# A five-layer transformer forward pass: order of score, transpose and pooled-product steps in three attention layers

## The chip, the cores and the metric

The kernel runs on one NeuronCore of a Trainium2 chip, as one launch. The metric is the device time of that launch in microseconds; the median of three runs counts. A profiled execution of the same program gives the trace.

## The reference

One sequence of 512 tokens, width 1024, float32, batch 1. Four layers come first, then one mixed layer with a feed-forward part:

```
for i in range(4):                        # attention kinds 0: MLA, 1: window, 2: fox, 0: MLA
    y = branch(x, ...)                    # (softmax attention * silu(gate)) @ w_out
    x = layernorm(8 ** 0.25 * x + y) * ln_g[i] + ln_b[i]
# fox: 16 heads of 64, causal
s = q @ k.T * 64 ** -0.5 + cum_q - cum_k  # cum: running sum of log_sigmoid(f + b)
# mixed layer
h = rmsnorm(x); z = h @ w_in
ya = b * causal_conv3(c * a)              # 256 channels
yb = pool_w @ (trailing mean(2, 4, 8, 16) - token) * pool_scale
yc = attention over the top 128 keys by a small indexer, 4 heads, relative bias
yd = attention over blocks (here: all causal keys), 4 heads, relative bias
x = x + rmsnorm(concat(ya, yb, yc, yd) @ w_out)
x = x + rmsnorm(swiglu(rmsnorm(x))); x = x + sigmoid(rmsnorm(x) @ wg) * (p @ wp)
```

The window layer (16 query heads, 4 key heads) sees 128 keys back and adds a per-head slope and a sink to the softmax.

## The kernel before

All activations stay on the chip. Each matrix is held as a rounded high part and a low part (`XTh`, `XTl` and so on), and each product is three products (high by high, low by high, high by low). Weights come in units of 512 KB at most: SyncE loads `w_raw`, ScalarE rounds it to `w_hi` (L1382), GpSimd subtracts to get `w_lo` (L2856). A "tile" is the product of one unit with the transposed tokens, 24 matmuls of 512 columns (L532), whose result goes to one of two projection banks in turn; ScalarE writes its high half, VectorE its low half, and only then is the bank free for the tile after next.

There is no scheduler. The program is written once for each engine, and each engine's list runs in the order in which it is written, with semaphores between them. A change of order on one engine must have its counterpart on the others.

Attention goes by pairs of heads, one head in each half of the array's rows. `pair_attention` on TensorE runs i from -2 to the last pair. In iteration i it takes the transposes of pair i, the scores of pair i+2, the product with V of pair i (`mix`, L772), and the layer's `fill(i, pos)`, which adds tiles for later pairs. The steps have numbers:

```
if n % 2:
    scores(i + 2, n // 2)
else:
    turn(i, n // 2)
```

`turn(i, ch)` (L758) transposes 14, 14 and 12 blocks of the probabilities into banks 4 and 5; it waits for the norm of these probabilities and for ScalarE's copy of the group before (L1537). `scores(i, ch)` (L716, and L728 for fox's bias rows, L732 for the mask of selected keys) writes two banks, 0 and 1 or 2 and 3 in turn, and waits with `ps_free` until VectorE has emptied the chunk before the last:

```
if c.sch >= 2:
    pe.wait_ge(ps_free, c.sch - 1)
```

A causal pair has three chunks: query rows 2 and 0 together, row 3, row 1 (with selection row 1 before row 3). In the window layer there are two chunks and two groups of transposes. `between(i)` says which steps come before the fills (a list) and which are woven into the tiles of fill 1 and 2 (a dictionary: point of weaving to steps; a tile has a point after every three matmuls, a value half after each eight). The third score chunk comes behind the fills, just ahead of `mix(i)`.

VectorE's `pair_attention` (L2206) empties a chunk with a custom operation that adds the bias and finds the maxima (L2227, `maxima`). The result goes to the buffer that pair i's probabilities lie in, so for the first chunk it waits, for each head, for pair i's transposes:

```
if ch == 0 and i >= 2:
    dve.wait_ge(pt_done, t_first[i - 2] + pr.turns_of(x))
```

`turns_of` is 2 for the first head and 3 for the second (1 and 2 in the window layer). Then come the norms of pair i+1 (L2254 and L2256; in the mixed layer only the reciprocal, L2252, and ScalarE does the multiplication, L1527), the gates (L2113), and the product of attention and gate (L2271). `norm_last` and `norm_first` move the second head's norm behind the fills and the mix, or ahead of them.

ScalarE takes in iteration i, in this order: copies of all groups of transposes of pair i (L1537), the high half of the output, exponentials of pair i+1, first head (L1512), a rounding of weights, second head, then norms and high halves of tiles. In the fox layer each score needs augmented rows (the running sums), moved by four small transfers from ScalarE's queue (L1892) right behind the gate tile of the iteration before; `scores` waits for them at its first chunk.

In the mixed layer `pooled(cc)` is a float32 product of the pooled channels (L1189) that waits for GpSimd's window sums (L2811 to L2820); VectorE scales it into `otmp` (L2698), ScalarE writes the high half and VectorE the low half. VectorE also finds the selected keys in rounds of eight (`top`, L2666 and L2667). In the condition `pairs[0].sel` the first pair is asked; only pairs 2 and 3 of the mixed layer select.

## Time and profile before

| | |
|---|---|
| runs | 1652.9 us median of 3 (1652.37 to 1653.56) |
| profiled execution | 1657.83 us |
| its span | 1656.0 us |
| mean granted TensorE clock | 0.995 |
| busy: TensorE, VectorE, ScalarE, GpSimd | 98%, 47%, 46%, 40% |
| chain that ended last: TensorE, VectorE, ScalarE | 80%, 11%, 5% |

The profile is one execution, seen by the hardware profiler. Times in its views are from the start of the span. A row of a timeline is a start, a duration, the engine with the line of the kernel, the operation, the tiles written and read, and in brackets how long the engine stood idle before it and who ended that. Matmuls overlap, so the distance between two starts is what one costs, not its duration. "PE" is TensorE, "DVE" VectorE, "ACT" ScalarE, "POOL" GpSimd; "ACTq" is ScalarE's queue issuing a transfer.

The fox layer's pairs lie between 470 and 700 us of the span, the window layer's between 280 and 415, the mixed layer's between 1099 and 1190.

### The profile page before, as it was taken

Reading aid. Unit: us, or ns where it says so; the run is one execution under the profiler, and the core shown is the slowest. Engines: PE = TensorE matmul, PEld = TensorE weight load, DVE = VectorE, ACT = ScalarE, POOL = GpSimd, SP = SyncE. Lnnn points to the kernel's source line nnn. Section 1 sums busy time; section 2 is a strip of 40 time slices with the busy share of each in tenths; the row PEclk is TensorE's granted clock in tenths of the full one; section 3 lists DMA queues with packets and bytes.
Section 4 is the critical chain, followed back from the end, with each engine's and each line's share of the span. In section 5 each row is a group of like instructions: output and inputs, shape, how many; then the busy total and the mean of one; then the engine's idle time right before and its main releaser. Section 6 shows DMA issues by size and latency. Waiting matters only on the chain.

```text
span 1656.0 us, 26230 instructions
## 1 busy us (share of the span) xinstructions
PE 1620.8 (98%) x10245; PEld 1313.5 (79%) x10245; DVE 776.0 (47%) x2044; ACT 757.8 (46%) x1465; POOL 658.2 (40%) x551
## 2 busy tenths in 40 slices
PE   8999999999999999999999999999999999999998
PEld 7777778887888787788777788777688888888877
DVE  3778635665543434354877464886051111001162
ACT  4566624655345444434576534328553322213252
POOL 5332234332443333243423243882235444444423
PEclk9999999999999999999999998999999999999999
DMA  6323144233452323153312265231243333333412
GB/s 174 71 45 87 52 161 125 80 83 60 160 157 55 85 56 93 58 194 79 88 41 75 73 184 152 79 90 56 90 135 102 102 91 101 102 92 97 120 62 89
DMA packets 216071, 161.32 MB, mean 97 GB/s; under 512 B 53763, under 2 KB 197155, under 8 KB 215948
## 3 DMA queue, kind: packets, MB, share of 16 engines
q1 hardware_dynamic: 205904, 130.21, 28.1%
q10 hardware_dynamic: 9820, 29.40, 5.7%
q8 instruction: 82, 1.34, 0.3%
q14 instruction: 41, 0.34, 0.1%
q0 software_dynamic: 224, 0.03, 0.1%
HBM read 148.32 MB, written 11.14 MB: 96 GB/s over the span
## 4 chain that ended last, share of the span: by engine, by line
PE 80%; DVE 11%; ACT 5%; issue 2%; POOL 2%; DMA 1%; SPq 0%; DVEq 0%; ACTq 0%; POOLq 0%
PE banks L532 40%; PE banks L483 8%; PE banks L485 7%; PE banks L484 7%; PE banks L772 4%; PE banks L716 4%; PE banks L614 4%; PE banks L758 3%; PE banks L738 1%; DVE banks L2354 1%; ACT AB L1512 1%; DVE banks L2343 1%; DVE AB L2356 1%; ACT w_hi L1382 1%; ACT G L1634 1%
## 5 line engine op out<-in xcount | busy, mean ns | idle before, releaser
L2856 POOL TENSOR_TENSOR w_lo<-w_raw,w_hi 128x512 fp32r<-128x512 f32 (+2 forms) x506 | 617.5, 1248 | 968.0 <-ACT w_hi L1382 967.7
L1382 ACT ACTIVATE w_hi<-w_raw 128x1024 fp32r<-128x1024 f32 (+4 forms) x254 | 249.8, 994 | 158.7 <-PE banks L485 102.0
L532 PE MATMUL banks<-XTh,w_hi 128*128 128x512 f32 (+5 forms) x1216 | 283.6, 375 | 7.2 <-DVE XTl L2316 3.0
L532 PE MATMUL banks<-XTl,w_hi 128*128 128x512 f32 (+5 forms) x1216 | 274.0, 367 | 0.0
L532 PE MATMUL banks<-XTh,w_lo 128*128 128x512 f32 (+5 forms) x1216 | 272.4, 367 | 0.0
L532 PEld LDWEIGHTS banks<-XTh,w_hi 128*128 128x128 f32 (+2 forms) x1216 | 209.0, 190 | 53.7 <-issue 8.3
L532 PEld LDWEIGHTS banks<-XTl,w_hi 128*128 128x128 f32 (+2 forms) x1216 | 212.7, 189 | 37.8
L532 PEld LDWEIGHTS banks<-XTh,w_lo 128*128 128x128 f32 (+2 forms) x1216 | 212.7, 189 | 37.4
L483 PE MATMUL banks<-w_hi,OTh 128*128 128x512 f32 (+1 forms) x448 | 172.8, 386 | 1.6 <-DVE QKl L2080 1.5
L484 PE MATMUL banks<-w_lo,OTh 128*128 128x512 f32 (+1 forms) x448 | 167.8, 375 | 0.0
L485 PE MATMUL banks<-w_hi,OTl 128*128 128x512 f32 (+1 forms) x448 | 167.7, 374 | 0.0
L1512 ACT ACTIVATE AB<-AB,nb 128x256 f32<-128x256 f32 (+3 forms) x288 | 152.5, 533 | 13.0 <-DVE nb L2237 13.0
L1537 ACT ACTIVATE AB<-banks 128x896 f32<-128x896 f32 (+1 forms) x100 | 89.0, 890 | 116.7 <-PE banks L758 116.7
L2256 DVE TENSOR_SCALAR_CACHE_REDUCE AB<-AB,ri 128x256 f32<-128x256 f32 (+3 forms) x256 | 118.2, 518 | 2.3
L2227 DVE CUSTOM_DVE_ANT_0 AB<-banks,zmask 128x384 f32<-128x384 f32 (+1 forms) x192 | 84.0, 487 | 58.2 <-PE banks L758 53.8
L2747 DVE TENSOR_TENSOR otmp<-banks,AB 128x512 f32<-128x512 f32 x22 | 15.2, 692 | 188.9 <-PE banks L532 188.9
L483 PEld LDWEIGHTS banks<-w_hi,OTh 128*128 128x128 f32 x448 | 84.2, 188 | 22.2 <-DVE QKl L2080 3.3
L2080 DVE TENSOR_TENSOR QKl<-banks,QKh 128x512 fp32r<-128x512 f32 (+2 forms) x80 | 54.4, 683 | 100.0 <-ACT QKh L1411 98.6
L485 PEld LDWEIGHTS banks<-w_hi,OTl 128*128 128x128 f32 x448 | 84.3, 188 | 15.5
L484 PEld LDWEIGHTS banks<-w_lo,OTh 128*128 128x128 f32 x448 | 84.4, 188 | 13.6
L1411 ACT ACTIVATE QKh<-banks 128x512 fp32r<-128x512 f32 (+2 forms) x80 | 46.8, 586 | 80.4 <-PE banks L532 64.5
L758 PEld LDWEIGHTS banks<-ident,AB 64*128 64x128 f32 x1344 | 50.4, 138 | 22.4 <-issue 19.7
(222 smaller groups left out, 2209.6 us busy)
## 6 DMA issues: line engine op xcount, KB each, us to landing
w_raw<-in_w_gate_up_dram SPq DMA_DIRECT2D x44, 512.0 KB, 3.8
w_raw<-in_fox_w_in_dram SPq DMA_DIRECT2D x30, 512.0 KB, 4.1
w_raw<-in_mla_w_in_dram SPq DMA_DIRECT2D x26, 512.0 KB, 4.9
w_raw<-in_w_in_dram SPq DMA_DIRECT2D x24, 512.0 KB, 4.0
w_raw<-in_w_down_dram SPq DMA_DIRECT2D x22, 512.0 KB, 3.6
w_raw<-in_swa_w_in_dram SPq DMA_DIRECT2D x20, 512.0 KB, 3.8
w_raw<-in_mla_w_out_dram SPq DMA_DIRECT2D x16, 512.0 KB, 3.2
x_spill<-AB ACTq DMA_DIRECT2D x16, 512.0 KB, 2.8
```

The source lines that it names most:

```text
L483: nc.tensor.matmul(o, ah, bh, start=first, stop=False, skip_group_check=True)
L484: nc.tensor.matmul(o, ah, bl, start=False, stop=False, skip_group_check=True)
L485: return nc.tensor.matmul(o, al, bh, start=False, stop=last, skip_group_check=True)
L532: mm = nc.tensor.matmul(o, wt[:, k, :], xt[:, k, lo:hi], start=first and n == 0 and k == 0, stop=last and n == 2 and k == nk - 1, skip_gro ...
L614: mm = nc.tensor.matmul(o[:, 256 * (t % 2):256 * (t % 2) + 256], xt[:, k, ts], parts[k // 4][low][:, k % 4, :], start=n == 0 and k == 0, s ...
L758: mm = nc.tensor.transpose(bank[4 + half][:, o:o + HD], SBP[a % 2][m // n][r, col:col + P], ident[r, r])
L1382: nc.scalar.activation(view(w_hi, u, RING), view(w_raw, u, RAW), ACT.Copy).then_inc(hi_done, 1)
L1512: ins = nc.scalar.activation(sc, sc, ACT.Exp, bias=nb[:, b, n0 + t:n0 + t + 1], scale=pr.scale, accum_out=rs[:, b, n0 + t:n0 + t + 1])
L1537: nc.scalar.activation(PTB[:, P * m0:P * m1].rearrange("p (n h q) -> p h n q", h=2, q=HD), banks[:, 4:6, 0:HD * n].rearrange("p h (n q) -> ...
L2227: ins = nc.vector.tensor_tensor_reduce(pr.score(b, x, t), o, pr.bias(t, x), 1.0, -3e38, ALU.add, ALU.max, mx[:, b, 4 * x + t:4 * x + t + 1])
L2256: ins = nc.vector.tensor_scalar(pr.score(b, x, t), pr.score(b, x, t), ri[:, b, 4 * x + t:4 * x + t + 1], None, ALU.mult, ALU.add, accum_ou ...
L2856: ins = pool.tensor_tensor(low[at], raw[at], high[at].bitcast(F32), ALU.subtract)
```

## The change

Six edits. (1) In `between`, fox pairs 0 to 5 take the second score chunk before the second group of transposes, and the third group of transposes and the third score chunk are woven into the first tile of the fills; a set keeps the third chunk from being issued twice. (2) The condition for the mixed layer asks the last pair, so that pairs 0 and 1 weave their second and third transposes and the second score chunk into a tile. (3) At the mixed layer's next to last pair the woven transposes come at points 1 and 2 instead of 2 and 4. (4) The second pooled product moves behind the query tile of pair 1 and the first two score chunks of pair 0, on TensorE, ScalarE and VectorE. (5) VectorE in the window layer does the second head's norm of i = 5 last. (6) A list holds the group count that the output product waits for.

```diff
--- before.py
+++ after.py
@@ -776,8 +776,12 @@
                     end(mm)
                     mixed_at[a] = c.g
 
+                scored = set()
+
                 def step(i, n):
 
+                    if n == 5:
+                        scored.add(i)
                     if n % 2:
                         scores(i + 2, n // 2)
                     else:
@@ -786,11 +790,13 @@
                 def between(i):
 
                     if i == n_pairs - 2:
-                        return [0], {2: [2], 4: [4]}
+                        return [0], {1: [2], 2: [4]} if pairs[i].sel else {2: [2], 4: [4]}
                     if pairs[0].window:
                         return ([0], {3: [2, 1, 3]}) if i == 0 else ([0, 1, 3, 2], {})
-                    if pairs[0].sel and i >= 0:
+                    if pairs[-1].sel and i >= 0:
                         return [0, 1], {1: [2, 3], 3: [4]}
+                    if pairs[0].aug is not None and 0 <= i < n_pairs - 2:
+                        return [0, 1, 3, 2], {2: [4, 5]}
                     return list(range(5)), {}
 
                 for i in range(-2, n_pairs):
@@ -825,7 +831,8 @@
                     fill(i, 2)
                     woven.pop()
                     assert i == n_pairs - 1 or not later
-                    scores(i + 2, 2)
+                    if i not in scored:
+                        scores(i + 2, 2)
                     mix(i)
                     fill(i, 3)
                 c.pair += n_pairs
@@ -1201,16 +1208,17 @@
             tile("pool")
             mark["pool", 1] = c.g
             pair_values(0)
-            pooled(1)
-            at_mixed = c.g
-
-            parts = []
+
+            parts, at_mixed = [], []
 
             def fill(i, pos):
                 if pos == 0:
                     if i < 1:
                         pair_tile("q", i + 3)
                 elif pos == 1:
+                    if i == -2:
+                        pooled(1)
+                        at_mixed.append(c.g)
                     if i < 1:
                         pair_tile("k", i + 3)
                     elif i == 1:
@@ -1231,7 +1239,7 @@
                 return OTh[:, OUT_ORDER[k], ts], OTl[:, OUT_ORDER[k], ts]
 
             def chunk_at(k):
-                return at_mixed if k < 4 else mixed_at[c.pair - 8 + k]
+                return at_mixed[0] if k < 4 else mixed_at[c.pair - 8 + k]
 
             pe.wait_ge(idx_r, 24)
             pair_attention(rel_pairs(), fill, mixed_ahead)
@@ -2009,15 +2017,16 @@
             hi(OTh[:, 2, :], otmp[:, :])
             pool_tile(1)
             value_units(1)
-            c.g += 1
-            groups_stored(act, c.g)
-            hi(OTh[:, 3, :], otmp[:, :])
 
             def fill(i, pos):
                 if pos == 0:
                     if i < 1:
                         pair_tile(i + 3)
                 elif pos == 1:
+                    if i == -2:
+                        c.g += 1
+                        groups_stored(act, c.g)
+                        hi(OTh[:, 3, :], otmp[:, :])
                     if i < 1:
                         pair_tile(i + 7)
                     elif i == 1:
@@ -2572,7 +2581,7 @@
                     gate(i + 1)
                     gate_at[i + 1] = c.g
 
-            pair_attention(swa_pairs(), fill, norm_first=(-1,))
+            pair_attention(swa_pairs(), fill, norm_last=(5,), norm_first=(-1,))
             ln_tail(1)
             for rows in (QKh, QKl):
                 for half in range(2):
@@ -2714,7 +2723,6 @@
             c.g += 1
             top(13)
             c.g += 2
-            pooled(1)
             dve.wait_ge(rel_in, 16 * 32)
             dve.wait_ge(x_out, 16 * T * 4)
 
@@ -2727,6 +2735,8 @@
                     elif i == 2:
                         c.g += 1
                 elif pos == 1:
+                    if i == -2:
+                        pooled(1)
                     if i < 0:
                         top(2)
                     if i < 1:
```

The order on TensorE, fox layer, one of the six pairs (L758 transposes, L716 and L728 scores, L532 the tile). Before:

```order
L728 MATMUL banks<-QKh 128x128 x2
L758 MATMUL banks<-ident,AB 128x64 x14
L716 MATMUL banks<-QKh 128x512 x2
L716 MATMUL banks<-QKl,QKh 128x512 x2
L716 MATMUL banks<-QKh,QKl 128x512 x2
L728 MATMUL banks<-QKh 128x512 x2
L758 MATMUL banks<-ident,AB 128x64 x12
L532 MATMUL banks<-XTh,w_hi 128x512 x8
```

and now:

```order
L728 MATMUL banks<-QKh 128x512 x2
L758 MATMUL banks<-ident,AB 128x64 x14
L532 MATMUL banks<-XTh,w_hi 128x512 x6
L758 MATMUL banks<-ident,AB 128x64 x12
L716 MATMUL banks<-QKh 128x256 x2
L716 MATMUL banks<-QKl,QKh 128x256 x2
L716 MATMUL banks<-QKh,QKl 128x256 x2
L728 MATMUL banks<-QKh 128x256 x2
L532 MATMUL banks<-XTh,w_hi 128x512 x2
```

The 12 transposes of the third group moved six matmuls into the tile, and the scores of 256 columns, which stood behind the tiles, follow them directly.

The order on TensorE, mixed layer, pair 0, from its second group of transposes on (L732 adds the mask of the selected keys):

```order
L532 MATMUL banks<-XTh,w_hi 128x512 x3
L758 MATMUL banks<-ident,AB 128x64 x14
L716 MATMUL banks<-QKh 128x256 x2
L716 MATMUL banks<-QKl,QKh 128x256 x2
L716 MATMUL banks<-QKh,QKl 128x256 x2
L732 MATMUL banks<-OTl,ident_r 128x256 x2
L532 MATMUL banks<-XTh,w_hi 128x512 x5
L532 MATMUL banks<-XTl,w_hi 128x512
L758 MATMUL banks<-ident,AB 128x64 x12
L532 MATMUL banks<-XTl,w_hi 128x512 x7
```

Before, both groups of transposes and the chunk between them stood ahead of the tile.

The order on VectorE, window layer, i = 5 (L2122 is the gate, L2280 the product of attention and gate, L2259 to L2265 the norm):

```order
L2122 SCALAR_TENSOR_TENSOR G<-G,banks 128x512
L2280 SCALAR_TENSOR_TENSOR otmp<-banks,G 128x512
L2259 TENSOR_TENSOR rs<-rs,es 128x4
L2263 RECIPROCAL ri<-rs 128x4
L2265 TENSOR_SCALAR AB,unused<-AB,ri 128x128
L2265 TENSOR_SCALAR AB,unused<-AB,ri 128x256 x3
```

Before, the last four of these rows stood ahead of the first two.

## Rows read from the trace of the kernel before

**Rows 1.** The page's first part: busy time of each engine (share of the span) and instructions.
```profile
PE 1620.8 (98%) x10245; PEld 1313.5 (79%) x10245; DVE 776.0 (47%) x2044; ACT 757.8 (46%) x1465; POOL 658.2 (40%) x551
```

**Rows 2.** List of waits of TensorE: waiter, releaser, us in total, times, longest.
```profile
PE banks L758 <- ACT AB L1537: 0.9, 3, 0.3
```

**Rows 3.** Timeline of TensorE, fox pairs 0 to 2: start us, us, engine, line, operation.
```profile
545.72 0.39 PE L716 MATMUL banks<-QKh 64*128 64x256 f32 x2
...
546.39 2.37 PE L772 MATMUL banks<-AB,V 128*64 128x512 f32 x16
548.69 0.65 PE L758 MATMUL banks<-ident,AB 64*128 64x64 f32 x14
549.22 0.44 PE L716 MATMUL banks<-QKh 64*128 64x384 f32 x2
...
551.66 0.41 PE L728 MATMUL banks<-QKl 64*128 64x512 f32 x2
552.20 0.59 PE L758 MATMUL banks<-ident,AB 64*128 64x64 f32 x12
552.72 2.11 PE L532 MATMUL banks<-XTh,w_hi 128*128 128x512 f32 x8
...
572.23 0.65 PE L758 MATMUL banks<-ident,AB 64*128 64x64 f32 x14
572.72 0.44 PE L716 MATMUL banks<-QKh 64*128 64x384 f32 x2
```

**Rows 4.** Timeline of VectorE in fox pair 1: S0's second half.
```profile
552.83 0.56 DVE L2227 CUSTOM_DVE_ANT_0 AB<-banks,zmask 128x384 f32<-128x384 f32 x1 [0.80 <-PE banks L758]
...
553.52 0.08 DVE L2227 DVE_READ_ACCUMULATOR2_ANT mx<- 128x1 f32 x1
```

**Rows 5.** Timeline of VectorE and TensorE at fox's first pairs: a score group that waits.
```profile
505.84 0.08 DVE L2227 DVE_READ_ACCUMULATOR2_ANT mx<- 128x1 f32 x1
...
505.98 0.50 PE L716 MATMUL banks<-QKh 64*128 64x512 f32 x2 [0.39 <-DVE mx L2227]
```

**Rows 6.** Timeline of ScalarE's queue: the last transfer of augmented rows of two pairs.
```profile
547.37 0.48 ACTq L1892 DMA_DIRECT2D QKl<-OTl  x1
...
570.91 0.48 ACTq L1892 DMA_DIRECT2D QKh<-OTl  x1
```

**Rows 7.** Timeline of VectorE and TensorE, sliding-window layer, i = 5 and 6.
```profile
391.42 0.54 DVE L2250 TENSOR_TENSOR rs<-rs,es 128x4 f32<-128x4 f32 x1 [1.03 <-ACT es L1515]
...
393.68 0.68 DVE L2113 SCALAR_TENSOR_TENSOR G<-G,banks 128x512 f32<-128x512 f32 x1
...
394.51 1.63 PE L532 MATMUL banks<-XTh,w_hi 128*128 128x512 f32 x6 [1.74 <-DVE G L2113]
396.07 0.65 PE L758 MATMUL banks<-ident,AB 64*128 64x64 f32 x14
```

**Rows 8.** Timeline of TensorE: the second pooled product.
```profile
1098.36 1.10 PE L1189 MATMUL banks<-AB 128*128 128x512 f32 x2 [1.31 <-POOL AB L2820]
```

**Rows 9.** Timeline of TensorE, ScalarE and VectorE, mixed layer, pairs 0 and 1.
```profile
1135.89 0.59 PE L758 MATMUL banks<-ident,AB 64*128 64x64 f32 x12 [0.27 <-ACT AB L1537]
...
1137.23 0.39 ACT L1512 ACTIVATE AB<-AB,nb 128x128 f32<-128x128 f32 x1
...
1142.71 1.92 ACT L1527 ACTIVATE AB<-AB,ri 128x128 f32<-128x128 f32 x4
1143.65 2.37 PE L772 MATMUL banks<-AB,V_odd 128*64 128x512 f32 x16
...
1145.22 0.69 DVE L2080 TENSOR_TENSOR QKl<-banks,QKh 128x512 fp32r<-128x512 f32 x1 [2.37 <-ACT QKh L1411]
...
1145.96 0.65 PE L758 MATMUL banks<-ident,AB 64*128 64x64 f32 x14
1146.42 0.42 PE L716 MATMUL banks<-QKh 64*128 64x384 f32 x2
...
1147.30 0.90 ACT L1537 ACTIVATE AB<-banks 128x896 f32<-128x896 f32 x1
```

**Rows 10.** Timeline of ScalarE and TensorE, mixed layer: the mix of pair 2.
```profile
1170.26 0.58 ACT L1434 ACTIVATE V<-banks 128x512 f32<-128x512 f32 x1
...
1170.93 3.88 PE L772 MATMUL banks<-AB,V 128*64 128x512 f32 x16 [2.45 <-issue]
```

**Rows 11.** Stretches: length, busy us (instructions) of PE, PEld, DVE, ACT, POOL; PEclk, DMA share, GB/s.
```profile
1001.00:1013.00 12.00, 12.00 (x59) 11.96 (x57) 2.87 (x5) 4.34 (x7) 5.01 (x4) 0.50 0.55 160
...
1171.00:1173.00 2.00, 2.00 (x6) 0.75 (x8) 0.00 (x0) 2.00 (x9) 1.93 (x2) 0.50 0.00 0
```

## Prediction

> **What bounds the kernel now.** I read the page first: TensorE is busy for 1620.8 us of 1656.0, 98% [rows 1]. So every gain is a TensorE wait removed, and every new TensorE wait is paid in full. The list of waits shows them small; the transposes that wait for ScalarE's copies lose 0.9 us in three places [rows 2]. Then I read timelines at the four places that the change touches. I call a pair's three groups of transposes T0, T1, T2 (steps 0, 2, 4 of pair i), the score chunks of pair i+2 S0, S1, S2 (steps 1, 3, and 5 or the call behind the fills), and the product with V "mix".
>
> In the fox layer TensorE never stands still for long: S2, mix, T0, S0, T1, S1, T2, then three tiles, one pair in 23.54 us from T0 to T0 (548.69 to 572.23) [rows 3]. What is to be seen there is who is close behind. S2 may start only when VectorE has emptied the banks of S0, the same two banks, since it waits for all score chunks but the last one. VectorE may empty the second head's half of S0 only when T2 is done, since it overwrites what T2 reads: its row at 552.83 starts after T2 and its last read ends at 553.60 [rows 4]. Today S2 comes 13 us later, so nobody notices. A score group that does wait for VectorE begins 0.06 us after such a read ends, 505.92 to 505.98 [rows 5]. And S0 of the next pair begins a fixed time after the last small ACT transfer of the augmented rows was issued: 547.37 to 549.22 and 570.91 to 572.72, that is 1.85 and 1.81 us [rows 3, 6]. So S0 already starts when that transfer lands. TensorE fills the 3.50 us from the end of the gate tile (545.72) to S0 with S2 (0.67), mix (2.30) and T0 (0.53) [rows 3].
>
> **The change part by part.**
>
> *Fox, six pairs (i = 0 to 5).* T0, S0, S1, T1, six matmuls of the first tile, T2, S2, rest. T2 is followed at once by S2. From T2's start VectorE begins 0.63 us later (552.20 to 552.83), needs 0.77 and wakes TensorE in 0.06: S2 starts 1.46 us after T2 instead of the 0.52 after which the tile now follows [rows 3 to 5]. That is 0.94 of new wait, six times. Back comes T2's present wait for ScalarE's copy of T1: S1's last two matmuls start at 551.66 and stream for some 0.23, T2 starts at 552.20, of which an ordinary switch is 0.1; I take 0.2 [rows 3]. The number of switches between tiles, scores and transposes stays eight a pair. T1 now leads into a tile; 12 transposes before a tile take 0.52, 14 before scores 0.46 [rows 3, 9], so I add 0.1. Net 0.94 - 0.2 + 0.1 = 0.84 a pair, 5.0 us for six. If VectorE were early by everything but its second half the wait would still be 0.7, if it had gated work ahead of it some 1.1: 3.6 to 6.6.
>
> Second, S2 no longer lies between the gate tile and the next S0. The transfers are issued from the same point, the end of the gate tile, so S0 stays 3.50 us behind it, and the 0.67 that S2 took there becomes idle time while S2's work is paid elsewhere. This holds for the pairs whose rows are fetched right before use and with no value tile between: after i = 0, 1, 3, 4. Four times 0.67 is 2.7 us; nothing at least, 3.2 at most. The Trainium skill, "DMA: Bandwidth & Descriptors", section "Anatomy of one DMA", gives some 2.0 us of fixed cost for a transfer on the GpSimd path; by that S0 would be held another 0.15 to 0.2 longer and the sum would be 0.7 higher. The rows have 1.85 and 1.81 for this queue, so they decide. Fox in sum: +7.7 us.
>
> *Sliding-window layer.* At i = 5 VectorE norms the second head before it finishes the gate (393.68), and TensorE's last gate tile waits 1.74 us for the bank at 394.51 [rows 7]. Now the gate comes first. The tile can start at about 392.75, behind T0, but T1 inside it (now 396.07) needs that norm, which starts behind the gate and the mix product at about 393.15 instead of 391.42 and still needs some 2 us: T1 at 395.2. Gain 0.9 of the 1.74; between 0.4 and 1.7. Queued behind the norm on VectorE is only the low half of the output, which waits for ScalarE anyway.
>
> *Second pooled product.* It waits 1.31 us for GpSimd's window sums at 1098.36 [rows 8]. Behind a query tile and two score chunks (over 7 us of work) the sums are done; the product itself moves and costs the same. VectorE's scale and subtraction move behind five selection rounds and the maxima; they are short and VectorE is the same length ahead of the selected scores. The key tile that follows now needs the bank of the query tile, which VectorE empties some 0.3 us before TensorE comes. -1.3, between -1.4 and -0.5.
>
> *Mixed layer, pairs 0 and 1.* The branch for them was dead before (it asked the first pair, which selects nothing) and lives now: T1 and S1 after three matmuls of the tile, T2 after nine. T2 of pair 0 comes 2.2 us later. But ScalarE copies all three groups before it turns to the next pair's exponentials, and it is busy without a break from T2's copy on: exponentials at 1137.23, norm 1142.71 for 1.92, so it needs 8.74 us from T2 (1135.89) to the norm at 1144.63, while TensorE's T0 of the next pair comes at 1145.96, 10.07 after T2 [rows 9]. With T2 2.2 later (and a switch more) TensorE is back after 8.0 and waits 0.8. S0 behind it waits for the low half of the key (1145.22 + 0.69, 10.0 us after T2) and loses another 0.8. At pair 1 the same shift costs T0 of pair 2 some 1.2, and its T1, now after one group of the value tile, waits for ScalarE's copy of T0, which ends about 11 us after the exponentials begin (1137.23 to 1148.20) [rows 9]: 1.9. The last mix, which waits 2.45 today because ScalarE's V copy at 1170.26 comes behind copies and exponentials [rows 10], is down to 0.7, since T2 of pair 2 comes two groups nearer to the tile's start. New waits 0.8 + 0.8 + 1.2 + 1.9 + 0.7 = 5.4, old ones 0.3 + 0.3 + 0.3 + 2.45 = 3.3, four more switches 0.6: +2.7, between -1.5 and +4.
>
> *The clock there.* In the stretch behind the 2.45 us of idling the granted clock is 0.50, the 1.2 GHz level, and the mix took 3.88 us instead of 2.37 at full clock [rows 9 to 11]. With the idle time cut into pieces I expect the clock to hold 2.4 GHz: -1.5. "TensorE: Matmul & The Clock Gate" of the Trainium skill, section "Part 1: The HAM clock gate", says that the clock follows how busy the engine was just before, not any one wait. By that rule two waits close together could bring it down as well, and the sum would be 1.5 higher; this is a rival below.
>
> **Sum.** +7.7 - 0.9 - 1.3 + 2.7 - 1.5 = +6.7 us. The profiled execution took 1657.8; it would be 1664.5. The runs' median is 1652.9, 4.9 below it, and the forecast for the median is 1659.6.
>
> **Rivals.** (1) *Fox as forecast, mixed pays off.* If ScalarE has more room than I give it, the mixed order costs nothing (-1.3 - 1.5 - 1) and the sum is about +3, 1656. For it: the old idle was 3.3 us and the longest piece shrinks. Against it: ScalarE has no gap in its rows there. (2) *The transfers hide.* Only the bank wait of S2 counts, fox +5.0: 1656.9. Against: the two equal distances of rows 3 and 6. (3) *Clock.* The waits of 1.2 and 1.9 us before T0 and T1 of pair 2 lie within 5 us and the clock falls there as it does today: +1.5, 1661.1. (4) *S2 never waits: not slower.* VectorE's emptying of S0 keeps up with TensorE. Its place is the start of S2 in the six fox pairs, its price the 0.94 each (5.6 in all), and it decides once the wait is under 0.3. The sum is then +1.1, 1654.0, no change that can be measured. For it: VectorE is idle before T2. Against: it can't begin before T2 ends, and the six matmuls of tile lie ahead of T2, not between T2 and S2. (5) *The slow stretch at 1000.* Between 1001 and 1013 the granted clock is 0.50 as well, behind short matmuls and small waits [rows 11]. If the later arrival kept the clock up there, half of that stretch, 6 us, would come back: +0.7, 1653.6. Against: the runs before agree within 1.2 us, so it falls there each time.
>
> **How the numbers follow.** Runs of this kernel spread by 1.2 us, so under 0.2% (3.3 us) I call it the same. Forecast 0.5, rival 1 0.13, rival 2 0.1, rival 3 0.12, rival 4 0.1, rival 5 0.05. Rival 1 lies on the bound: 0.045 of it counts as slower, 0.065 as the same, 0.02 as faster. Of the forecast 0.02 ends within the bound. Rival 4 is 0.06 the same and 0.04 faster, where the transfers hide too; rival 5 is the same. Rounded: slower 0.74, same 0.19, faster 0.07. The range takes in all but rivals 4 and 5 and the far ends: the fox bounds alone reach from 3.6 to 9.8, the others shift that by -3 to +1; 1654.5 to 1662.5.
>
> **What would show it.** In the timeline of fox pairs: T2's first transpose to S2's first matmul 1.4 to 1.5 us with VectorE's maxima as releaser, and T0 to S0 1.2 us after i = 0, 1, 3, 4, with a period of 25.0 us instead of 23.5. In the window layer the wait of 1.74 gone and one of under 1 us before T1. The pooled product without a wait. Mixed: TensorE waits before T0 and S0 of the later pairs and before T1 of pair 2, ScalarE without gaps, clock 1.0 at the last mix. The forecast is wrong if S2 follows T2 within 0.6 us or the fox period is not over 24 us.

## The result and the profile after

The changed kernel is slower. In the runs taken together with the result its median is 1665.1 us against 1652.8 (four runs each; ratio 1.0074, 95% interval 1.0050 to 1.0098). Those four runs lie in two pairs, 1661.7 and 1661.9, 1668.2 and 1668.4. With eight more executions (last experiments) the median of twelve is 1662.1: seven lie at 1659.9 to 1662.2, five at 1668.1 to 1668.5. The prediction was 1659.6 with 1662.5 as its upper end.

The page's busy line, beside [rows 1], says little: TensorE is busy 3.2 us longer in a span that is 10.6 us longer (1666.6 against 1656.0).

```profile
PE 1624.0 (97%) x10245; PEld 1316.4 (79%) x10245; DVE 773.8 (46%) x2044; ACT 757.7 (45%) x1465; POOL 658.8 (40%) x551
```

The list of TensorE's waits says more (waiter, releaser, us in total, times, longest). The wait for VectorE's maxima was there once before, for 0.4 us, that for ScalarE's copies with 0.9 us in total, and that of the mix (L772) was longer, 2.5 us; the others are new:

```profile
PE banks L716 <- DVE mx L2236: 5.6, 7, 0.9
...
PE banks L758 <- ACT AB L1545: 1.9, 1, 1.9
...
PE banks L772 <- issue: 1.7, 1, 1.7
PE banks L716 <- DMA QKl<-OTl: 1.5, 2, 1.0
PE banks L758 <- ACT AB L1535: 1.5, 2, 1.1
...
PE banks L716 <- DMA QKh<-OTl: 1.2, 2, 0.7
...
PE banks L758 <- DVE AB L2265: 0.8, 1, 0.8
...
PE banks L716 <- DVE QKl L2089: 0.6, 1, 0.6
```

The timeline of TensorE in fox pair 1, which answers to [rows 3]:

```profile
546.46 2.38 PE L772 MATMUL banks<-AB,V 128*64 128x512 f32 x16
548.77 0.65 PE L758 MATMUL banks<-ident,AB 64*128 64x64 f32 x14
550.38 0.44 PE L716 MATMUL banks<-QKh 64*128 64x384 f32 x2 [0.96 <-DMA QKl<-OTl]
...
554.67 0.58 PE L758 MATMUL banks<-ident,AB 64*128 64x64 f32 x12
556.13 0.39 PE L716 MATMUL banks<-QKh 64*128 64x256 f32 x2 [0.88 <-DVE mx L2236]
...
574.33 0.65 PE L758 MATMUL banks<-ident,AB 64*128 64x64 f32 x14
575.51 0.44 PE L716 MATMUL banks<-QKh 64*128 64x384 f32 x2 [0.53 <-DMA QKh<-OTl]
```

From T2 (554.67) to S2 (556.13) it is 1.46 us, and the releaser is VectorE. From T0 to S0 it is 1.61 and 1.18 us, where it was 0.53 and 0.49. The period is 25.56 us instead of 23.54. VectorE's own rows answer to [rows 4]: it begins the second half 0.63 us after T2 starts, and its last read ends 0.05 us before S2.

```profile
555.30 0.56 DVE L2236 CUSTOM_DVE_ANT_0 AB<-banks,zmask 128x384 f32<-128x384 f32 x1 [1.22 <-PE banks L758]
...
555.99 0.09 DVE L2236 DVE_READ_ACCUMULATOR2_ANT mx<- 128x1 f32 x1
```

The last transfers of augmented rows, which answer to [rows 6], are issued at 548.11 and 573.67; S0 follows 2.27 and 1.84 us behind:

```profile
548.11 0.48 ACTq L1900 DMA_DIRECT2D QKl<-OTl  x1
...
573.67 0.48 ACTq L1900 DMA_DIRECT2D QKh<-OTl  x1
```

In the sliding-window layer the wait of 1.74 us is gone and one of 0.76 stands before T1 [rows 7]; the pooled product now runs without a wait [rows 8]:

```profile
392.87 1.63 PE L532 MATMUL banks<-XTh,w_hi 128*128 128x512 f32 x6
395.25 0.65 PE L758 MATMUL banks<-ident,AB 64*128 64x64 f32 x14 [0.76 <-DVE AB L2265]
...
1113.70 1.12 PE L1196 MATMUL banks<-AB 128*128 128x512 f32 x2
```

The mixed layer's pairs, TensorE's rows with their waits, beside [rows 9, 10]:

```profile
1154.19 0.65 PE L758 MATMUL banks<-ident,AB 64*128 64x64 f32 x14 [0.37 <-ACT AB L1535]
1155.46 0.44 PE L716 MATMUL banks<-QKh 64*128 64x384 f32 x2 [0.63 <-DVE QKl L2089]
...
1169.90 0.65 PE L758 MATMUL banks<-ident,AB 64*128 64x64 f32 x14 [1.10 <-ACT AB L1535]
...
1173.57 0.79 PE L758 MATMUL banks<-ident,AB 64*128 64x64 f32 x14 [1.88 <-ACT AB L1545]
...
1183.03 2.38 PE L772 MATMUL banks<-AB,V 128*64 128x512 f32 x16 [1.74 <-issue]
```

Two stretches run at 1.2 GHz, as in [rows 11], but the first is longer and the second lies elsewhere: 17.1 us from 1006.7 on (13.7 us from 999.9 on before), and 3.4 us at T1 of pair 2 instead of at the last mix (the starts and lengths are those of the trace's record of the granted clock; the rows lie inside them; stretch: length, busy us of PE, PEld, DVE, ACT, POOL; PEclk, DMA share, GB/s).

```profile
1007.00:1023.00 16.00, 16.00 (x87) 15.77 (x87) 2.87 (x5) 4.34 (x7) 4.99 (x4) 0.50 0.50 144
1174.00:1177.00 3.00, 3.00 (x27) 2.66 (x24) 0.00 (x0) 0.92 (x1) 0.00 (x0) 0.50 0.00 0
```

**Where the 10.6 us came in**, by the same point of the program in both traces:

| from, to | before, us | after, us | difference |
|---|---|---|---|
| start to T0 of fox pair 0 | 525.14 | 524.33 | -0.8 |
| to T0 of fox pair 6 | 153.78 | 162.33 | +8.6 |
| to the indexer's first scores (3.4 us more at half clock) | 340.81 | 342.49 | +1.7 |
| to T0 of mixed pair 0 (the pooled product is in here) | 112.42 | 110.93 | -1.5 |
| to the first transposes behind the last mix | 45.58 | 48.21 | +2.6 |

The sum is +10.6; behind the last point nothing changes. The first line contains the window layer; the executions of one kernel differ by some 0.7 us there (525.04 in a second trace of the changed kernel), so its -0.8 is good to about that.

### The profile page after: what moved, and what is told of

Same layout as the page of the kernel before. It is cut to its first block, busy times and chain, and to the rows that moved or that the text cites. A ratio compares the mean times of both kernels' runs of the same rounds, so it can differ in the third digit from the quotient of the medians.

```text
span 1666.6 us, 26230 instructions
## 1 busy us (share of the span) xinstructions
PE 1624.0 (97%) x10245; PEld 1316.4 (79%) x10245; DVE 773.8 (46%) x2044; ACT 757.7 (45%) x1465; POOL 658.8 (40%) x551
## 4 chain that ended last, share of the span: by engine, by line
PE 80%; DVE 10%; ACT 5%; issue 2%; DMA 1%; POOL 1%; ACTq 0%; SPq 0%; DVEq 0%; POOLq 0%
PE banks L532 41%; PE banks L483 8%; PE banks L485 7%; PE banks L484 7%; PE banks L716 4%; PE banks L614 4%; PE banks L772 3%; PE banks L758 3%; ACT AB L1520 1%; PE banks L738 1%; DVE banks L2363 1%; DVE banks L2352 1%; DVE AB L2365 1%; ACT w_hi L1390 1%; ACT G L1642 1%
## 5 line engine op out<-in xcount | busy, mean ns | idle before, releaser
L532 PE MATMUL banks<-XTh,w_hi 128*128 128x512 f32 (+5 forms) x1216 | 284.9, 376 | 5.5 <-DVE XTl L2325 3.0
L532 PE MATMUL banks<-XTl,w_hi 128*128 128x512 f32 (+5 forms) x1216 | 275.1, 368 | 0.0
L532 PE MATMUL banks<-XTh,w_lo 128*128 128x512 f32 (+5 forms) x1216 | 273.3, 368 | 0.0
L532 PEld LDWEIGHTS banks<-XTh,w_hi 128*128 128x128 f32 (+2 forms) x1216 | 208.4, 190 | 51.8 <-issue 6.6
L532 PEld LDWEIGHTS banks<-XTh,w_lo 128*128 128x128 f32 (+2 forms) x1216 | 213.7, 190 | 37.4
L532 PEld LDWEIGHTS banks<-XTl,w_hi 128*128 128x128 f32 (+2 forms) x1216 | 213.2, 190 | 38.0
L2265 DVE TENSOR_SCALAR_CACHE_REDUCE AB<-AB,ri 128x256 f32<-128x256 f32 (+3 forms) x256 | 118.2, 518 | 2.3
L758 PEld LDWEIGHTS banks<-ident,AB 64*128 64x128 f32 x1344 | 51.3, 139 | 25.2 <-issue 19.3
```

What stands on the lines that cost most here:

```text
L532: mm = nc.tensor.matmul(o, wt[:, k, :], xt[:, k, lo:hi], start=first and n == 0 and k == 0, stop=last and n == 2 and k == nk - 1, skip_gro ...
L758: mm = nc.tensor.transpose(bank[4 + half][:, o:o + HD], SBP[a % 2][m // n][r, col:col + P], ident[r, r])
L2265: ins = nc.vector.tensor_scalar(pr.score(b, x, t), pr.score(b, x, t), ri[:, b, 4 * x + t:4 * x + t + 1], None, ALU.mult, ALU.add, accum_ou ...
```

## Experiments

**The fox order alone, and everything but it.** The new fox order was put into the kernel before:

```diff
+                    if pairs[0].aug is not None and 0 <= i < n_pairs - 2:
+                        return [0, 1, 3, 2], {2: [4, 5]}
...
-                    scores(i + 2, 2)
+                    if i not in scored:
+                        scores(i + 2, 2)
```

> The kernel before with the new order of the fox layer alone (the pooled product, the sliding-window layer and the mixed layer as before). Theory: the fox layer carries nearly all of the loss, about +8.5 us against before: six waits of S2 for VectorE's emptying of S0's banks (T2 to S2 1.45 us instead of 0.52, some 5.4 us) and a longer idle time before the next S0 behind four pairs (some 3.2 us). Rival A (the mixed layer's new order is the larger part): not over +5. Rival B (the whole loss is the granted clock of the mixed layer, which only reacts to a later arrival): the fox rows show waits, but the time comes out within 3 us of before.

Measured: 1668.2 us against 1653.0 (ratio 1.0074, interval 1.0052 to 1.0096; here and below the ratio is the recorded one over all executions, which with two levels is not the quotient of the medians); five of six executions at 1668.1 to 1669.1, one at 1660.9. In its trace T0 of pair 0 to T0 of pair 6 takes 162.22 us, +8.4, with the same waits. Taking the two lines out of the changed kernel was the counterpart:

> The changed kernel with the fox layer in its old order. Theory: the window layer gives 0.8 back, the pooled product 1.3, the mixed pairs cost 2.7: +0.6 us against before, between -1 and +2. Rival A (mixed layer is the larger part): +4 to +6.

Measured: 1652.7 against 1653.0 (interval 0.9982 to 1.0012). The rest of the change comes out even within this interval, though not by the forecast parts: in this trace the mixed part takes 49.45 us, +3.9, with the clock at 1.2 GHz for 6.8 us of it. Rivals A and B are out: the fox layer carries the larger part of the loss in rows of its own, and with the fox order alone the mixed part is what it was (45.66 us).

**The two fox costs taken apart.** In the first version S2 comes late in the tile, in the second it goes back between the gate tile and the mix:

```diff
-                        return [0, 1, 3, 2], {2: [4, 5]}
+                        return [0, 1, 3, 2], {2: [4], 5: [5]}
```

> The kernel before with the new fox order, but S2 behind 15 matmuls of the first tile instead of right behind T2 (6 matmuls). Theory: VectorE has emptied the banks by then, so the six waits of 0.87 us are gone; S2 still does not lie between the gate tile and the next S0, so the idle time before S0 of 1.2 to 1.6 us stays in four pairs: +3 us against before, between +2 and +4.5. Rival C (both losses come from T1 standing behind S0 and S1, which puts ScalarE and VectorE late): +7 or more, as with the full order.

```diff
-                        return [0, 1, 3, 2], {2: [4, 5]}
+                        return [0, 1, 3, 2], {2: [4]}
```

> The kernel before with T0, S0, S1, T1 and then T2 inside the first tile, but S2 in its old place between the gate tile and the product with V. Theory: neither the bank wait nor the longer idle time before S0, and T2's old wait of 0.2 us for ScalarE's copy is gone: -1 us against before, between -2 and +0.5. Rival C: +4 or more.

S2 late: the fox part takes 158.39 us, 3.8 less than with the full order and 4.6 more than before. All waits of the six pairs for VectorE's maxima are gone; what is left there is in the list of waits of this stretch:

```profile
PE banks L716 <- DMA QKh<-OTl: 1.4, 2, 0.8
PE banks L716 <- DMA QKl<-OTl: 1.1, 2, 0.5
PE banks L614 <- ACT w_hi L1389: 0.6, 1, 0.6
```

So the transfers are exposed in four pairs with no bank wait about. +3 was expected and +4.6 came: 2.5 are the idle time for the transfers, 0.6 is a weight copy that is late for a value tile, and the last 1.5 falls to what is left, among it one more switch into and out of a tile in each of six pairs; that share was not measured apart. S2 in its old place: fox takes 155.68 us, +1.9, where I expected -1. No bank wait, but one transfer that lands late (1.1 us, behind i = 3) and the weight copy (0.8). The sign is right (rival C is out), the size was not: the order of T1, S1 and T2 gains nothing. The medians of these two, 1662.8 and 1662.6, are of no use for this, since 7 and 10 of their 12 executions lie on a high level, of which more below; their low executions (1655.4 to 1657.9, and 1654.4 and 1654.8) agree with the traces.

**The parts of the mixed layer.** First the order of pairs 0 and 1 alone, then pair 2's alone, in the kernel before:

```diff
-                    if pairs[0].sel and i >= 0:
+                    if pairs[-1].sel and i >= 0:
```

> The kernel before with only the new order of the mixed layer's pairs 0 and 1 (T1, S1 and T2 inside the query tile and the key tile), pair 2 as before. Theory: ScalarE is behind, so T0 and S0 of pair 1 wait 0.4 and 0.6 us and T0 of pair 2 waits 1.1: the part from T0 of pair 0 to T0 behind the last mix grows by 1.5 to 3 us against before. Rival D (the cost lies in pair 2's earlier T1 alone): this part does not grow by over 0.5 us.

```diff
-                        return [0], {2: [2], 4: [4]}
+                        return [0], {1: [2], 2: [4]} if pairs[i].sel else {2: [2], 4: [4]}
```

> The kernel before with only pair 2 of the mixed layer in its new order (T1 after one group of the value tile, T2 after two). Theory: ScalarE's weight split stands ahead of its V copy and waits for the value tile's last product, so the last mix still waits 1.7 us instead of 2.45; T1 waits under 0.5 us since T0 is not late here: this part shrinks by 0.3 to 1 us. Rival E (the weight split is not what holds it, the earlier T2 makes the V copy early): wait at the last mix 0.7 us or less, the clock stays at 1.0 there, -3 us.

Pairs 0 and 1: the part takes 48.27 us against 45.58, +2.7, with waits of 0.36, 0.63, 1.10 and 0.92 us before T0, S0, T0, T1 and still 2.45 before the last mix; the median is 1655.6 against 1652.9. Rival D is out: this edit has the whole cost of the mixed layer in these traces. Pair 2 (median 1656.4, seven of twelve executions high; ratio 0.9998, interval 0.9981 to 1.0015): 43.61 us, 2.0 less, but in this execution the clock held and the mix took 2.38 instead of 3.88 us, so the order itself gives some 0.5. The wait at the last mix is 1.74, as expected.

**Pooled product and window layer alone**, the edits as in the change:

> The kernel before with only the second pooled product moved and the gate ahead of the norm in the sliding-window layer. Theory: -0.8 (window layer) and -1.5 (pooled product), so 2.3 us faster than before where the granted clock falls as often. Rival F (the pooled move only shifts the wait into the key tile behind it): -0.8.

Measured: 1648.9 against 1652.9 (ratio 0.9969, interval 0.9953 to 0.9985), faster than both kernels, and by 1.7 us more than the two edits are worth. The stretch at the last mix, after the same wait of 2.45 us, has most of it:

```profile
1163.00:1167.00 4.00, 3.64 (x22) 2.38 (x23) 0.18 (x1) 4.00 (x13) 2.36 (x2) 1.00 0.21 38
```

The granted clock is 1.00 here and was 0.50 in [rows 11], and the mixed part takes 44.04 us instead of 45.58. One and the same wait brings the clock down in one execution and not in another. The window layer may add to it: behind its old wait of 1.74 us before the gate tile the clock falls for 3.4 us in four of the nine traces that have this wait (the fox order alone, T2 alone, pair 2 alone, the delayed kernel below), and T0 of fox pair 0 then comes some 1.1 us later; in none of the eight traces with the new order there does it fall. Nine and eight traces are too few to call this shown.

**What holds the last mix.** ScalarE's V copy comes behind a weight split that reuses a buffer of the value tile. I tried to exchange the two in the layer's fill:

```diff
                     elif i == 1:
-                        advance()
                         values(0)
+                        advance()
```

> A version that might beat both: the kernel before with the pooled product moved, the gate ahead of the norm, pair 2 of the mixed layer in its new order, and ScalarE's V copy of that pair put ahead of the weight split. Theory (the weight split sets the last mix's wait): that wait falls from 1.7 to about 0.6 us, the clock holds 2.4 GHz there, and with the other two parts the kernel is 4 to 6 us faster than before. Rival E (the split is not what holds it): the wait at the last mix is the same as with the order of pair 2 alone, and the time 2.5 us under before.

Measured: 1648.5 us, and the wait is still 1.74. The order on ScalarE there had not moved:

```profile
1161.38 1.06 ACT L1383 ACTIVATE w_hi<-w_raw 128x1024 fp32r<-128x1024 f32 x1 [1.10 <-PE banks L614]
1162.35 0.58 ACT L1435 ACTIVATE V<-banks 128x512 f32<-128x512 f32 x1
```

The split is issued by the pair's own steps. So that was changed instead:

```diff
-                    if not c.early and 0 <= i < n_pairs - 1:
+                    if not c.early and 0 <= i < n_pairs - 1 and not (pairs[i].sel and i == n_pairs - 2):
                         early()
```

> The version with the pooled product moved, the gate ahead of the norm and pair 2 of the mixed layer in its new order (no new fox order, pairs 0 and 1 as before), and now ScalarE's weight split of that pair really behind its V copy: the split is issued inside the pair's own steps, so exchanging it with the copy in the fill had moved nothing. Theory (the split, which waits for the value tile's last product and takes 1.06 us, sets the start of the last mix): the wait there falls from 1.74 to 0.8 us and the part from T0 of pair 0 to T0 behind the last mix from 43.6 to 42.6 us. Rival E (something else holds the mix): 1.74 us as before.

The V copy now starts when the value tile ends and the mix waits 0.73 us (timelines of ScalarE and TensorE):

```profile
1160.44 0.60 ACT L1435 ACTIVATE V<-banks 128x512 f32<-128x512 f32 x1 [1.03 <-PE banks L614]
1160.93 1.05 ACT L1383 ACTIVATE w_hi<-w_raw 128x1024 fp32r<-128x1024 f32 x1
...
1161.14 2.37 PE L772 MATMUL banks<-AB,V 128*64 128x512 f32 x16 [0.73 <-issue]
```

The part takes 42.56 us instead of 43.61, as expected. Right behind it 0.59 of this is lost again: T1 of the last pair now waits for ScalarE's copy of T0 (1168.16), which comes behind a norm of 3.72 us and is no earlier than TensorE. The median is 1647.8 against 1652.8 (ratio 0.9972, interval 0.9956 to 0.9987), 0.6 below the version before it, a difference that 11 and 8 executions don't clear of noise.

**The two levels.** Each version so far has executions some 5 to 8 us above the others, with a mean granted clock of 0.992 to 0.996 instead of 0.997 to 1.000. In the seven traces of high ones the stretch at half clock near 1005 us is there, in the ten others not. Two tests: does a later arrival alone change how often it falls, and do the waits ahead of it cause it?

```diff
+                for _ in range(again):
+                    nc.tensor.matmul(o, h[:, 0, :], XTh[:, 0, lo:hi], start=True, stop=False, skip_group_check=True)
...
-                    tile("gate")
+                    tile("gate", again=8 if i == -1 else 0)
```

> The kernel before with eight matmuls of the first fox gate tile repeated (its first matmul, same operands and same result, start flag set each time), so that everything behind it comes 1.8 us later and nothing else changes. It tests why the stretch of half clock near 1000 us appears in some executions and not in others. Theory G (it is chance in relation to the time of arrival, so the fox order raises its share only by coming later): about +1.8 us on the fast executions, and the share of executions that lie 5 to 7 us higher differs clearly from the kernel before's, near the 10 of 12 of the version with T2 alone moved, whose fox layer was 1.9 us longer. Rival H (the fox order itself does it): the share stays near the kernel before's 16 of 60.

```diff
-                for _ in range(3):
-                    open_half("iq", P)
+                for n in range(3):
+                    open_half("iq", P, again=4 if n == 2 else 0)
                 turn(2)
-                open_half("ik")
+                open_half("ik", again=9)
```

> The changed kernel with the TensorE waits at the start of the mixed layer filled: in the layer's early column groups the first matmul of the third and of the fourth group (256 columns) is repeated 4 and 9 times with the same operands, which takes the place of the waits of 0.56 and 1.20 us there. Theory (those waits, together with the short matmuls, pull the clock down): the half-clock stretch of 13 to 17 us near 1005 is gone in nearly all executions and the median lies at the changed kernel's lower level, 1661 to 1662 us. Rival J (the short matmuls alone do it, or something outside the kernel): the share of high executions is as in the changed kernel.

> The changed kernel itself once more, to have more executions of it beside the others: two levels as in its first four runs, about 1661.8 and 1668.3 us, with over half of the executions on the higher one.

> The kernel before with the two waits at the start of the mixed layer filled by repeated matmuls as in the filled version of the changed kernel. Theory (the waits pull the clock down there in some executions): the kernel before lay 5 to 8 us high in 22 of 86 executions; here none or one of 12 does, the rest at 1650.4 to 1653.8 as before. Rival J (the waits have nothing to do with it): about 3 of 12 high.

> The kernel before with the new fox order alone, waits at the start of the mixed layer filled. With the waits it lay on the high level in 5 of 6 executions (1668.1 to 1669.1), once at 1660.9. Theory: none or one of 12 high, the median at 1660 to 1661.5, so the fox order costs 8 us in work and waits and the rest of its 15 us was the clock. Rival H (the fox order itself causes the high level, wherever the clock falls): over half of the executions near 1668.

> The fastest version so far (pooled product moved, gate ahead of the norm, pair 2 in its new order, V copy ahead of the weight split; 1646.8 to 1648.6 in 8 executions and 1652.7 to 1653.2 in 3) with the waits filled. Theory: the high level goes, median 1647 to 1648, none above 1650. Rival J: 3 of 12 at 1653 as without.

| version | executions on the high level | median, us |
|---|---|---|
| before | 27 of 111 | 1652.7 to 1653.0 |
| changed kernel with the old fox order | 2 of 12 | 1652.7 |
| order of pairs 0 and 1 alone | 4 of 12 | 1655.6 |
| order of pair 2 alone | 7 of 12 | 1656.4 |
| pooled product and window layer alone | 2 of 12 | 1648.9 |
| these two and pair 2's order | 2 of 8 | 1648.5 |
| before, delayed by 1.8 us in fox | 7 of 12 | 1661.0 |
| before, waits filled | 0 of 12 | 1652.9 |
| fox order alone | 5 of 6 | 1668.2 |
| fox with S2 late | 7 of 12 | 1662.8 |
| fox with S2 in its old place | 10 of 12 | 1662.6 |
| fox order alone, waits filled | 0 of 10 | 1659.5 |
| changed kernel | 5 of 12 | 1662.1 |
| changed kernel, waits filled | 0 of 6 | 1661.8 |
| fastest version without fox order | 3 of 11 | 1647.8 |
| the same, waits filled | 0 of 10 | 1647.1 |

The stretch of 20 us at this place in the fox order alone, and in the same with the waits filled:

```profile
1005.00:1025.00 20.00, 18.79 (x111) 18.31 (x110) 6.15 (x10) 5.78 (x10) 4.99 (x4) 0.61 0.42 119
```

```profile
1005.00:1025.00 20.00, 19.69 (x164) 18.52 (x162) 8.68 (x14) 10.96 (x22) 9.55 (x8) 1.00 0.49 136
```

TensorE gets through 164 matmuls in it instead of 111; the repeated ones lie ahead of this stretch. And in the filled one the wait of 1.20 us has shrunk to 0.16, since VectorE sets its end and not TensorE (timeline of TensorE, kernel before with the waits filled):

```profile
993.43 1.27 PE L529 MATMUL banks<-XTh,w_hi 128*72 128x256 f32 x9
...
997.68 1.11 PE L534 MATMUL banks<-XTh,w_hi 128*128 128x128 f32 x8 [0.16 <-DVE XTl L2318]
```

The four versions have no high execution in 38 with the waits filled, and 40 in 140 without. So the waits of 0.56 and 1.20 us are shown to be needed for the fall; they were filled together, and which of them counts was not tried. Rival J is out, and so is rival H of the filled fox version: with the waits filled no execution at 1668 is left. The medians put the fox order at 6.6 to 6.8 us then (1659.5 against 1652.9 filled and 1652.7 unfilled). The two filled traces, in which the clock does not fall at all before the last microseconds, have 7.8 us between their spans (1656.5 and 1648.7).

What raises the share is not shown. The versions with the fox order, whole or in part, had 27 of 42, those without it and without the delay 20 of 67, the kernel before 27 of 111. The delay alone (the low executions at 1653.5 to 1654.1, the high ones at 1659.8 to 1663.1) had 7 of 12. That would fit a share that goes by when the kernel arrives. But pair 2's order alone, which changes nothing ahead of this place, had 7 of 12 as well, so the delay's twelve executions can't tell the arrival from chance, nor from the fox order itself.

The second trace of the changed kernel (1662.1 us, without the stretch near 1005) also shows what the first one hid. Its fox part takes 161.94 us and its mixed part 49.44, where the first had 162.33 and 48.21; around T1 of pair 2 the clock is down for 6.8 us instead of 3.4:

```profile
1166.00:1172.00 6.00, 5.96 (x44) 5.53 (x45) 0.00 (x0) 2.99 (x7) 0.00 (x0) 0.50 0.00 0
```

The changed kernel with its waits filled has the same (49.44). Against the kernel before the mixed part is 3.9 us longer by this, and 5.4 us against its filled trace, where the clock held at the last mix (44.02).

The last version, 1647.1 against 1652.7 (ratio 0.9965, interval 0.9953 to 0.9978), is the fastest of all. It is the change without its fox order and without the order of pairs 0 and 1, with ScalarE's split behind the V copy and the waits filled.

## Why the prediction was wrong in size and right in sign

**Fox: right, a little small.** +7.7 was forecast, +8.6 came (+8.2 in the second trace of the changed kernel). The bank wait was as described: T2 to S2 1.45 to 1.47 us in all six pairs, VectorE the releaser. The four distances from T0 to S0 grew by 3.2 us in sum where the step had 2.7; the one of 2.27 us behind the last issue made most of the difference. The 2.0 us of fixed cost that the Trainium skill gives for the GpSimd path ("DMA: Bandwidth & Descriptors", "Anatomy of one DMA") lies between the 1.84 and the 2.27 us that this trace has from issue to S0 on ScalarE's queue; by it the sum would have been 0.7 higher, nearer to what came. The rest, 5.4 against 5.0, is the net of 0.84 a pair, which was 0.90. Rivals 2 (the transfers hide) and 4 (S2 never waits) are out.

**Window layer and pooled product: right.** -0.9 and -1.3 forecast, -0.8 and -1.5 measured.

**Mixed pairs: the sum right in the profiled pair, the parts not.** +2.7 forecast, +2.6 measured there. T0, S0, T0 and T1 were to wait 0.8, 0.8, 1.2 and 1.9 us; they waited 0.37, 0.63, 1.10 and 1.88. The last mix was to wait 0.7 and waited 1.74: the step "T2 of pair 2 comes two groups nearer" counted copies and exponentials and left out the weight split, which can't start before the value tile ends. No row shows the 0.6 for four more switches either, at 0.15 each where the fox layer was given 0.1. That the sum fits is in part luck. Rival 1 (mixed pays off) is out.

**The clock at the last mix, -1.5: wrong.** It fell all the same, 5 us earlier at T1 of pair 2, behind the waits of 1.10 and 1.88 us: rival 3, to which I had given 0.12. The sum with it would have been 8.2. In the second trace the fall there is twice as long, 6.8 us, and the mixed part 3.9 us longer than before instead of the 1.2 forecast. The rule of the Trainium skill, "TensorE: Matmul & The Clock Gate", "Part 1: The HAM clock gate", that the clock follows how busy the engine was just before, spoke for this rival, and both traces agree.

**The slow stretch at 1000: the step that failed most.** Rival 5 was argued away by "the runs before agree within 1.2 us, so it falls there each time". The opposite was so. The three runs agreed because they all lay on the low level; the profiled execution, 4.9 us above their median, was the one that had it, and the text treated this distance as a constant. In about a quarter of the executions of the kernel before it falls. Some 6 us hang on it, nearly as much as on the fox order, and the sum had no term for it. In the changed kernel it fell in two of the first four runs (1668.2 and 1668.4; the other two 1661.7 and 1661.9), and in five of all twelve. With a term for it the range would have reached to 1668. The range was also narrower than its own parts, 3.6 - 3 to 9.8 + 1, which give 1653.5 to 1663.7.

In the profiled pair, where the stretch falls in both, the forecast was +6.7 and +10.6 came: the fox term's 0.9, the clock's 1.5 at the mixed layer, and 1.7 for a longer stretch near 1000, less 0.2 elsewhere. On the low level 1661.7, the median of the seven low executions, stands against 1652.7, +9.0. The trace of a low execution puts the miss there mostly in the clock of the mixed layer (+3.9 for that part instead of +1.2) and little in fox; how the short falls of the clock mix in the two medians is not known execution by execution. The other 3 us of the first median, 1665.1, against the median of twelve, 1662.1, are the luck of two executions in four on the high level.

## What to carry to other kernels

A score group that is pulled forward to fill TensorE must find its bank emptied: before moving it, count from the last transposes that the emptying has to wait for, not from the scores. And look at what the moved work covered in its old place, since a transfer behind it becomes visible. Where the profiled execution lies several us above the runs, find the stretch that makes the difference before costing anything; if it is a fall of the clock behind small waits, repeating a matmul into the bank that is about to be written fills the wait at no cost that was measured here and takes the upper level away (the low one keeps its width, 1650.4 to 1653.7 in the kernel before).

## What was unexpected of the hardware

The granted clock does not belong to the program: the same wait of 2.45 us before the last mix was followed by 1.2 GHz in one trace and by 2.4 GHz in another (pooled product and window layer alone, where the row above has 1.00), and the same 1.20 us near 1000 in some executions and not in others. Of the nine traces with those 2.45 us the clock was down in the mix in five (3.3 to 4.1 us for 16 matmuls) and up in four (2.4 us). No single wait of TensorE ahead of any of these falls was longer than 2.45 us. The Trainium skill, "TensorE: Matmul & The Clock Gate", "Part 1: The HAM clock gate", says that the monitor runs freely, so that one kernel meets it in a different phase in each run; that the long stretch falls in 27 of 111 executions of the kernel before agrees with it, and no run here shows the phase itself. And some 1.6 us of repeated matmuls (13 of 256 columns, an estimate from the 0.12 us that one costs in the row of L529) in place of waits added nothing to the kernel before (1652.9 against 1652.7, interval 0.9979 to 1.0006).
